# A decoder step on one core: other orders of work at the two borders of a feed-forward product done with seven block products

## What is computed

```python
x = x + 0.5 * swiglu(rmsnorm(x, ffn1_norm), ffn1_w_gate, ffn1_w_up, ffn1_w_down)
h = rmsnorm(x, mix_norm)
...   # mLSTM branch and differential attention, gated and merged
x = x + merged @ w_out
x = x + 0.5 * swiglu(rmsnorm(x, ffn2_norm), ffn2_w_gate, ffn2_w_up, ffn2_w_down)
# swiglu(x, g, u, d) = (silu(x @ g) * (x @ u)) @ d,  D_FF = 2816
```

## Time and profile before

| | us |
|---|---|
| median of three runs | 1666.86 (1666.51 to 1668.64) |
| the profiled execution's own time | 1664.32 |
| its span, first to last instruction | 1662.5 |
| TensorE busy | 1612.4 (97%) |
| VectorE busy | 891.5 (54%) |
| ScalarE busy | 630.0 (38%) |
| chain that ended last, TensorE's share | 89% |
| seven-product stage, from its first matmul to the first of the down product | 1261.88 to 1510.93 |

### The profile page before, as it was taken

The page is one execution under the profiler, slowest core; times in us unless marked ns, Lnnn a source line. Parts: engine busy times, 40 slices in busy tenths (PEclk is TensorE's granted clock), DMA queues, the critical chain, the costliest instruction groups (busy, mean ns, idle before and its releaser), DMA issues.

```text
span 1662.5 us, 30294 instructions
## 1 busy us (share of the span) xinstructions
PE 1612.4 (97%) x12544; PEld 1529.6 (92%) x12544; DVE 891.5 (54%) x1410; ACT 630.0 (38%) x992; POOL 4.5 (0%) x20
## 2 busy tenths in 40 slices
PE   8999999999999989999999999999997999999997
PEld 7999999999998668999999976679997999998997
DVE  4333333243593443553336679674456888886333
ACT  5222222222333433542211148573245555554223
POOL 0000000000000000000000000000000000000000
PEclk9999999999999999999999999999999999999999
DMA  5322233332232471223333341453322333323221
GB/s 130 92 88 78 87 88 92 94 88 82 67 102 55 169 255 39 75 81 86 103 92 100 88 163 51 160 196 88 89 77 76 102 103 102 102 77 105 82 81 67
DMA packets 247512, 164.34 MB, mean 99 GB/s; under 512 B 9054, under 2 KB 230483, under 8 KB 247418
## 3 DMA queue, kind: packets, MB, share of 16 engines
q1 hardware_dynamic: 247128, 162.46, 33.2%
q10 hardware_dynamic: 290, 0.57, 0.1%
HBM read 145.43 MB, written 16.42 MB: 97 GB/s over the span
## 4 chain that ended last, share of the span: by engine, by line
PE 89%; DVE 4%; ACT 2%; DMA 2%; issue 1%; SPq 1%; DVEq 0%; ACTq 0%
PE ps L439 58%; PE ps L1598 14%; PE ps L903 3%; PE ps L1121 2%; PE ps L1085 1%; PE ps L1321 1%; PE ps L1272 1%; PE ps L983 1%; PE ps L1391 1%; DVE small L2700 1%; PE ps L1170 1%; PE ps L1482 1%; PE ps L1435 1%; PE ps L1510 1%; PE ps L1318 1%
## 5 line engine op out<-in xcount | busy, mean ns | idle before, releaser
L439 PE MATMUL ps<-xn_hi,w_hi 128*128 128x280 f32 (+1 forms) x1520 | 440.7, 290 | 2.4 <-DVE w_lo L411 1.6
L439 PE MATMUL ps<-xn_hi,w_lo 128*128 128x280 f32 (+1 forms) x1520 | 442.2, 291 | 0.0
L439 PE MATMUL ps<-xn_lo,w_hi 128*128 128x280 f32 (+1 forms) x1520 | 440.6, 290 | 0.0
L407 ACT ACTIVATE w_hi<-raw 128x1024 fp32r<-128x1024 f32 (+1 forms) x154 | 173.3, 1126 | 616.5 <-PE ps L439 608.3
L411 DVE TENSOR_TENSOR w_lo<-raw,w_hi 128x1024 fp32r<-128x1024 f32 (+1 forms) x154 | 201.2, 1307 | 184.4 <-ACT w_hi L407 184.2
L439 PEld LDWEIGHTS ps<-xn_hi,w_hi 128*128 128x128 f32 x1520 | 286.2, 188 | 3.5 <-DVE w_lo L411 2.2
L439 PEld LDWEIGHTS ps<-xn_hi,w_lo 128*128 128x128 f32 x1520 | 286.0, 188 | 0.0
L439 PEld LDWEIGHTS ps<-xn_lo,w_hi 128*128 128x128 f32 x1520 | 285.4, 188 | 0.0
L439 PE MATMUL ps<-h_hi,w_hi 128*128 128x280 f32 (+1 forms) x660 | 193.2, 293 | 2.9 <-DVE h_lo L2963 2.9
L439 PE MATMUL ps<-h_hi,w_lo 128*128 128x280 f32 (+1 forms) x660 | 192.0, 291 | 0.0
L439 PE MATMUL ps<-h_lo,w_hi 128*128 128x280 f32 (+1 forms) x660 | 191.3, 290 | 0.0
(11 more groups left out here) (450 smaller groups left out, 3114.4 us busy)
## 6 DMA issues: line engine op xcount, KB each, us to landing
raw<-in_w_in SPq DMA_DIRECT2D x55, 512.0 KB, 3.7
raw<-in_ffn_w_down SPq DMA_DIRECT2D x32, 704.0 KB, 4.5
raw<-in_ffn_w_gate SPq DMA_DIRECT2D x22, 512.0 KB, 3.8
raw<-in_ffn_w_up SPq DMA_DIRECT2D x22, 512.0 KB, 3.7
rawg<-in_ffn_w_gate SPq DMA_DIRECT2D x44, 256.0 KB
rawu<-in_ffn_w_up SPq DMA_DIRECT2D x44, 256.0 KB, 4.0
Cb<-in_state_C SPq DMA_DIRECT2D x32, 256.0 KB, 3.8
out<-Cb SPq DMA_DIRECT2D x32, 256.0 KB, 2.7
```

Of the source, the lines that this page charges most:

```text
L407: act.activation(w_hi[s][:, 0:p.nk, :], raw[s][:, 0:p.nk, :], ACT.Copy).then_inc(hi_done[s], 1)
L439: mm = pe.matmul(ps[:, bank + half, 0:p.half], w[s][:, k, :], x[:, k0 + k, cols], start=first and k == 0 and a == 0, stop=last and k == p. ...
```

## The change

The lists of all three engines are rewritten at the borders; the number of matmuls and of their columns stays. Start: VectorE forms panel 0's weight sums before the squares and X of the last tile, the last square is added last, and `norm` moves behind P6 of panel 0; the Ln, Exp and Silu table move behind ScalarE's first work for panel 1, and VectorE waits for them in panel 1 (`gate_norm`). P5 of panel 0 starts on the first three pairs while the last is made. In each panel P5 stands ahead of P6. Loads: one DMA for gate and one for up instead of two each, which swaps the two halves of U. End: three hidden tiles are split before ScalarE's `second_sum(21)`, five more before panel 21's last gate, at new places in `h_hi` (`place`); the first down tile goes over the 22 k tiles with both column halves at each.

```diff
+        def place(k):
+            return (k + 14) % FT
...
             def raw_panel(p, j):
-                for two in range(2):
-                    sp.dma_start(rawg[:, :, two, :], wg[:, :, two, :]).then_inc(in_g7.sem, 16)
+                sp.dma_start(rawg[:, :, :, :].rearrange("p k two n -> p (k two) n"), wg).then_inc(in_g7.sem, 16)
...
-                for two in range(2):
-                    sp.dma_start(rawu[j % 2][:, :, two, :], wu[:, :, 1 - two, :]).then_inc(in_u7[j % 2].sem, 16)
+                sp.dma_start(rawu[j % 2][:, :, :, :].rearrange("p k two n -> p (k two) n"), wu).then_inc(in_u7[j % 2].sem, 16)
...
             def strassen(j):
...
-                    early, rest = range(DT // 2 - 1), range(DT // 2 - 1, DT // 2)
-                    for k in early:
+                    end_k = DT // 2 - 1
+                    for k in range(end_k):
                         more(pe, xl_done, 3 * k + 1)
-                    seventh(a11, 0, c, early, first=True)
-                    seventh(a12, 2, c + 2, early, first=True)
-                    norm(2, up2, (3, 7))
-                    more(pe, xl_done, 3 * (DT // 2) - 2)
-                    seventh(a11, 0, c, rest).then_inc(product7.sem, 1)
-                    seventh(a12, 2, c + 2, rest).then_inc(product7.sem, 1)
-                    more(pe, xl_done, 3 * (DT // 2))
+                        seventh(a11, 0, c, (k,), first=True)
+                        seventh(a12, 2, c + 2, (k,), first=True)
+                    after(pe, lo7, LO7, "s31", j)
+                    for k in range(end_k):
+                        more(pe, xl_done, 3 * k + 2)
+                        seventh(s1, 3, c + 1, (k,), first=True)
+                    more(pe, xl_done, 3 * end_k + 1)
+                    seventh(a11, 0, c, (end_k,), first=True).then_inc(product7.sem, 1)
+                    seventh(a12, 2, c + 2, (end_k,), first=True).then_inc(product7.sem, 1)
+                    more(pe, xl_done, 3 * end_k + 2)
+                    seventh(s1, 3, c + 1, (end_k,), first=True)
+                    more(pe, xl_done, 3 * end_k + 3)
+                if j >= 1:
+                    after(pe, lo7, LO7, "s31", j)
+                    if j >= 2:
+                        after(pe, gate7, GATE7, "g2", j - 2)
+                    seventh(s1, 3, c + 1, first=True)
                 after(pe, lo7, LO7, "s2", j)
                 after(pe, part7, PART7, "r1", j)
                 seventh(s2, 6, c).then_inc(product7.sem, 1)
-                after(pe, lo7, LO7, "s31", j)
-                if j >= 2:
-                    after(pe, gate7, GATE7, "g2", j - 2)
-                seventh(s1, 3, c + 1, first=True)
                 if j >= 1:
                     last()
+                else:
+                    norm(2, up2, (3, 7))
...
+            def down_first(p, u):
+                after(pe, hidden7, HIDDEN7, "h1", FT - 2)
+                after(pe, gate7, GATE7, "g2", FT - 2)
+                for s in range(2):
+                    pe.wait_ge(lo_done[s], p.before + 1)
+                    for k in range(s * KD, s * KD + KD):
+                        pe.wait_ge(tile_lo, u.lo0 + k + 1)
+                        for half in range(2):
...
+                    mm.then_inc(mm_done[s], 1)
...
             def operands_hi(k):
                 more(act, w4_ready, 2 * k + 2)
                 copy(XH[:, k, 0:3, 0:n7], W4[:, 1:4, 0:n7]).then_inc(xh_done.sem, 1)
+                if k == DT // 2 - 1:
+                    square(2, DT - 1, c7)
...
             first_sum(0)
-            rms(2, up2, 4)
+            u_split(0)
+            g_split(1)
+            second_sum(0)
+            s2_split(1)
+            u_split(1)
+            third_sum(0)
+            s31_split(1)
+            first_sum(1)
+            rms(2, up2, (3, 7))
             act.activation(small[0:1, 60:61], con[0:1, 0:1], ACT.Silu)
-            u_split(0)
-            for j in range(FT):
-                if j >= 1:
+            gate(0, "g1", late7)
+            for j in range(1, FT):
+                if j >= 2:
                     first_sum(j)
                 if j + 1 < FT:
                     g_split(j + 1)
                 gate(j, "g1", late7)
+                if j + 1 == FT:
+                    after(act, product7, PRODUCT7, "p2", j)
+                    for k in range(3):
+                        h_split(k)
                 second_sum(j)
...
             split_hi(act, down2, 0, 0)
+            for k in range(3, 8):
+                h_split(k)
             gate(FT - 1, "g2", early7)
-            for k in range(KD):
-                h_split(k)
             split_hi(act, down2, 0, 1)
-            for k in range(KD, FT):
+            for k in range(8, FT):
                 h_split(k)
...
+                    if j == DT // 2 - 1 and s == 0:
+                        sums_31(0)
+                        sum_2(0)
                     if s == 0:
                         squares(2, 2 * j, c7)
                     if j == DT // 2 - 1 and s == 0:
-                        sums_31(0)
-                        sum_2(0)
+                        sum_4(0)
                         g_rest(0)
+                    if j == DT // 2 - 1 and s == 1:
                         s31_rest(0)
                 operands(j)
-
-            v.wait_ge(rn_ready, 3)
-            v.tensor_scalar(rh[:, c7:], rn[:, c7:], 0.5, None, ALU.mult)
+            s2_rest(0)
+            squares(2, DT - 1, c7)
...
             for j in range(FT):
                 if j >= 1:
                     up_sum(j - 1)
-                else:
-                    sum_4(0)
-                    s2_rest(0)
                 u_rest(j)
...
+                if j == 1:
+                    v.wait_ge(rn_ready, 3)
+                    v.tensor_scalar(rh[:, c7:], rn[:, c7:], 0.5, None, ALU.mult)
+                    gate_norm(0, "g1", late7)
                 gate_1(j)
...
+            for k in range(3):
+                h_rest(k)
             up_sum(FT - 1)
             hidden_2(FT - 2)
             split_lo(v, down2, 0, 0)
+            for k in range(3, 6):
+                h_rest(k)
             hidden_1(FT - 1)
+            for k in range(6, 8):
+                h_rest(k)
             gate_2(FT - 1)
             hidden_2(FT - 1)
-            for k in range(KD):
-                h_rest(k)
             split_lo(v, down2, 0, 1)
-            for k in range(KD, FT):
+            for k in range(8, FT):
                 h_rest(k)
```

More of the change, by code:

```diff
@@ L426, in first_product, with product @@
                     mm.then_inc(mm_done[s], 1)
-        def product(pe, p, j, s, bank, x_hi, x_lo, k0=0, first=True, last=True, tiles=None, tile_at=None, rest=None):
+        def product(pe, p, j, s, bank, x_hi, x_lo, k0=0, first=True, last=True, tiles=None, tile_at=None, rest=None, at=None):
             pe.wait_ge(lo_done[s], j + (p.before + 1))
@@ L438, in product @@
                     for a, (w, x) in enumerate(((w_hi, x_hi), (w_hi, x_lo), (w_lo, x_hi))):
-                        mm = pe.matmul(ps[:, bank + half, 0:p.half], w[s][:, k, :], x[:, k0 + k, cols],
+                        i = at(k0 + k) if at is not None and x is h_hi else k0 + k
+                        mm = pe.matmul(ps[:, bank + half, 0:p.half], w[s][:, k, :], x[:, i, cols],
                                        start=first and k == 0 and a == 0,
@@ L869, in raw_panel @@
             def raw_panel(p, j):
-                wg, wu = (w[:, 128 * j:128 * j + 128].rearrange("(k two p) n -> p k two n", two=2, p=128) for w in p.w)
+                wg, wu = (panel(w, 0, DT, 128 * j) for w in p.w)
                 if j == 0:
@@ L993, in down_last @@
             def down_last(p, u):
-                for i in range(DT - 1):
-                    down_tile(p, u, i // 2, i % 2, tiles=tile_lo if i == 0 else None)
+                for i in range(1, DT - 1):
+                    down_tile(p, u, i // 2, i % 2, at=place)
                     if i >= 1:
@@ L1674, in _ @@
             rest_of(FT - 1)()
+            def down_first(p, u):
[6 more added lines that the diff above has]
+                        for half in range(2):
+                            cols = slice(p.c0 + half * p.half, p.c0 + (half + 1) * p.half)
+                            for a, (w, x, i) in enumerate(((w_hi, h_hi, place(k)), (w_hi, h_lo, k), (w_lo, h_hi, place(k)))):
+                                mm = pe.matmul(ps[:, half, 0:p.half], w[s][:, k - s * KD, :], x[:, i, cols],
+                                               start=k == 0 and a == 0, stop=k == FT - 1 and a == 2)
+                    mm.then_inc(mm_done[s], 1)
+            down_first(down2, up2)
             down_last(down2, up2)
@@ L1700, in mixed_tile, with rms @@
                 tile(1, i)
-            def rms(r, p, step=1):
+            def rms(r, p, banks=None):
                 act.wait_ge(nm_full, r + 1)
-                act.activation(tok(rn, p), ps[:, 5 - step:6:step, 0:p.half] if step == 1 else ps[:, 3:8:step, 0:p.half], ACT.Ln, bias=con[:, C_EPS:C_EPS + 1],
```

(25 more changed lines are left out.)

26 lines of the change are left out of this document (17 added, 9 removed).

## The result

The changed kernel took 1654.6 us (median of four runs, 1651.61 to 1656.42) beside 1667.75 us for the kernel before; the ratio is 0.9919, 95% interval 0.99 to 0.9937. Executions far out of line (2249 us in e5, 2630 in e7, whose profile it was, 4050 for a run of before beside e12) are left out everywhere. The profiled execution took 1656.42 us; its span is 1654.6.

The account below looks back on a forecast made before the run. TensorE, 97% busy, bounds the kernel, with gains only at the borders. Start 9.3, minus 2.6 and 0.3 given back, plus end 3.5 gives 9.9, say 10.0 us: 1666.9 to 1656.9 us, range 1653.5 to 1661.5.

Parts of the forecast that it names:

- The start: First border, up to P1 of panel 1: P1(1) starts at 1273.1 instead of 1282.5, 9.3 us gained.
- The DMAs: Gate and up weight loads: one DMA instead of two for each matrix brings panel 0's data 0.2 us earlier.
- Half the clock at the start: First border, after the 5.8 us wait: clock at 0.50 for most of 5.5 us, expected to go.
- the price of a rival: Last border: the clock falls in the new 2.3 us gap, costing 1.4 us, total 1658.4; chance 0.13.
- Given back in panels 1 and 2: After the moved Ln, Exp and tables: P7(1) waits 1.2 us, P5(2) 1.0, P5(1) 0.2, restarts 0.2; together 2.6 lost.
- The 0.3 us held back for panels 3 to 5: Panels 3 to 5: cover for P5's earlier need of S31 may be thin, so another 0.3 us taken off.
- the rival with 4 us more on ScalarE: Panel 1: Ln, Exp and tables hold ScalarE longer, delaying P7(1); 4 us more give 1661; chance 0.07.
- P5 ahead of P6: Steady panels: P5 wants S31 one product (1.5 us) earlier, within the slack; priced at nothing.
- The rival with 1.0 us in each of 20 panels: Panels after 1: VectorE never catches up, P5 waits 1.0 us in each, total 1676; chance 0.03.
- The end: P3(21) to second down tile: eight tiles run at once, then a 2.3 us wait; 3.5 us gained.

Follow-up runs that it names:

- e5: The changed kernel as it is, timed in more rounds beside more runs of before: 1654.05 us against 1665.43, ratio 0.9941.
- e7: The changed kernel with gate and up loaded by two DMAs each again, the halves of U still swapped: ratio 0.9939.
- e12: The changed kernel with P6 ahead of P5 again in panels 1 to 21 and another split order at the end, second run: 1651.53 us, ratio 0.9902.
- e2: The changed kernel with the end of the kernel before, so the new start without the new end: 1659.41 us, ratio 0.9956.
- e11: The kernel before with one move on VectorE, sum_4(0) and s2_rest(0) ahead of the wait for rn: 1664.41 us, ratio 0.9987.
- e9: The changed kernel with gate and up loaded by two DMAs each again, a repeat of e7: ratio 0.993, stage 264.29 us.
- e1: The kernel before, unchanged, profiled once more: stage 274.72 us, profile span 1668.2 us.
- e3: The kernel before with the changed end alone: 1662.19 us, ratio 0.9969.
- e4: The kernel before with P5 ahead of P6 in every panel and nothing else: 1668.14 us, ratio 1.0018.
- e6: The changed kernel with P6 ahead of P5 again in panels 1 to 21: 1655.27 us, ratio 0.9937.
- e8: The changed kernel with gate_2(21) ahead of two h_rest, and hidden tiles 8 to 10 ahead of the second weight half's split: 1654.34 us, ratio 0.9935.
- e10: The changed kernel with P6 ahead of P5 again in panels 1 to 21 and another split order at the end, first run: 1654.09 us, ratio 0.9923.

## Why the prediction was right, point by point

- **The start.** 9.55 us against 9.3. The rows came out nearly where the lists had put them: P1(1) 17.4 us after the first X (forecast 17.15), G's low part the last to come for it, with a wait of 1.0 (forecast 1.2). e2 shows that this part stands alone. e11 shows why moving one piece was not enough: three things stood behind Ln, Exp and the tables at once; with S2's low part and the load moved ahead of them, the wait moved to the third, `second_sum`. The moves inside the start were not run one by one, so how the 9.55 us divide among them is read from the rows, not measured.
- **The DMAs.** The forecast took 0.2 us for the merge; it brought 0.14. The data were used 5.7 us after the first issue, as in panel 1 of before, and not 5.4; P1(1) was 0.2 us later than forecast. The Trainium skill (DMA: Bandwidth & Descriptors, section "Anatomy of one DMA") states a fixed cost of about 2 us for each DMA on the path from GpSimd; an estimate from it, with the DMAs added up one after another, gives 4 us for the merge. These are issued by SyncE, and e9 shows that four in flight together don't add up so: 5.88 us for all of them.
- **Half the clock at the start.** I counted it among the losses of before. In the first profile it was covered: P1(1) waited for the weights of panel 1, which were loaded only after `sum_4(0)`, so the slow matmuls of P6, P5 and P7 ran inside that wait. e1 agrees, where a clock that came back 0.9 us earlier only made the wait longer. e11 took that load away, and with it the cover: there the slow P7(0) delayed P1(1). Where the clock falls earlier (e3) or stays down into panel 1 (e4), it costs the old start 1.6 and 1.0 us more.
- **Half the clock at the end.** The prediction read 16 matmuls for 27 behind the wait of 2.9 us as a loss and took 1.4 us from it as the price of a rival. In the old end it cost nothing, because TensorE there follows the `h_rest` at 0.64 us a tile. The clock stood at half for 3.4 us in before, e1 and e2, for 6.8 in e11 and not at all in e4, and from P4(21) to the second down tile these took 25.75, 25.74, 25.76, 25.76 and 25.72 us. TensorE's windows behind the wait, of e11 and of e4:

```profile
1514.70:1520.50 5.80, 5.79 (x25) 0.50 0.09 27
...
1512.20:1519.00 6.80, 6.76 (x34) 1.00 0.11 33
```

What it would cost in the new end no run shows. The rival's low chance also leaned on the 2.4 us wait before `norm`, behind which the clock had held. That was one execution: in e3 and e11 it was down before that same wait ended, in e4 1.5 us after it. Behind the 1.9 us wait that the new end left, it held in all five traces that have it (after, e3, e5, e6, e9).
- **Given back in panels 1 and 2.** P7(1) waited 1.26 us (forecast 1.2), P5(2) 0.8 (1.0), P5(1) has no listed wait (0.2). From P1(1) to P1(3) it took 23.93 us after and 21.15 before: 2.8 us given back, where the forecast had 2.6. Beyond the waits that is 0.7 us, and the forecast had counted 0.2 for starting up again. The 0.3 us held back for panels 3 to 5 was not needed. That the table has 2.5 is luck: from P1(3) to P4(21) it took 200.47 us instead of 200.74, with one wait of 0.6 us in each, because the matmuls followed each other a little faster (last section). The three table loads cost their 1.28 us each (the load at 1279.21, `rn` from 1280.51), so the rival with 4 us more on ScalarE is out. The Trainium skill (ScalarE: Activation LUTs, section "What ACT_TABLE_LOAD costs") adds a drain of about 1.38 us to each load. These rows don't show it: 0.02 us of idle time stand between the load's end and `rn`.
- **P5 ahead of P6.** Nothing in the steady panels, as forecast, for S31's low part had its slack. The rival with 1.0 us in each of 20 panels is out in after and in e4. The exchange itself is a loss of 1.0 us in panels 1 and 2 (e6).
- **The end.** 3.4 us against 3.5. The wait for the ninth hidden tile was 1.9 us, not 2.3 (the prediction's own times, 1514.0 and 1516.1, give 2.1). It ended nearly where the forecast had it, 11.5 us after P4(21); it was shorter because TensorE was done with the first eight tiles later, at 9.6 and not at 9.2. The clock did not fall behind it.
- **The total.** The sum was 10.0 and the traces say 10.5, of which 0.3 is the spacing that nobody had forecast; the rest is terms that were off by 0.1 to 0.5 us either way. The forecast median of 1656.9 is 2.3 us above 1654.6 and 2.9 above the 1654.05 of e5, within what medians of four and five runs scatter.

## What to carry to other kernels

When several engines' lists stand behind one slow step (here Ln, Exp and three table loads), moving the work that releases the longest wait brings little (0.6 us at P1(1) for a wait of 5.8, e11): write down what each engine has behind the step, and move the step itself to where every engine has other work. An addition of durations along the three lists, checked first against the order that exists (it was 0.4 us off), forecast each new wait to within 0.4 us. And at a border between two stages, order the splits by when their first reader comes: operands whose weights are already there go ahead of the next weights' split (with an earlier `gate_2`, 1.8 us, e8).

## What the runs showed of the hardware that was not expected

- The spacing of matmuls differs between kernels whose steady panels hold the same instructions. Steady panels of 84 matmuls without a wait took 10.53 us in the kernel before, e1 and e6, 10.51 in the change, e2, e4, e5, e8 and e9, and 10.47 in e3, e10, e11 and e12. It was the same, to 0.01 us, in both executions of each kernel that was profiled twice (before and e1; the change and e5; e10 and e12), and e1 to e4, run on one chip, show all three values. Between e6 and e10 no instruction of those panels differs. From P1(3) to P4(21) that is 200.74 us in e6 and 199.73 in e10: 1.0 us, as much as an exchange of products. Its cause was not tried and stays open. Where two stages are compared, this part has to be taken out first.
- The clock at half rate came at another place of the work from execution to execution. Counted from the first X, it fell at 16.7 us in before and 15.8 in e1, for 6.8 us each; in e3 and e11 at 10.4 for 3.4, and again at 17.3 and 20.7 for 6.8; in e4 at 12.3 for 3.4, and again at 19.2 for 10.2, into panel 1. Each of e3, e4 and e11 was profiled once, so what of this is the kernel's and what the execution's is open.
